# Last mixture of experts: weights in 4 MB units of 32768-byte rows in four slots

## The reference

```
h    = normalised tokens (512 x 1024), modulated by a scale and a shift per feature
for e in 16 experts:                       # 64 tokens each
    a    = h[tokens of e]                  # 64 x 1024
    hid  = silu(a @ w1[e]) * (a @ w3[e])   # w1, w3: 1024 x 2048 (8 MB each)
    y    = hid @ w2[e]                     # w2: 2048 x 1024 (8 MB)
    out[tokens of e] += gate * y
```

## Time and profile before

| | us |
|---|---|
| runs shown | 2056.22, 2057.51, 2052.18 |
| their median | 2056.22 |
| the profiled execution | 2052.67 |
| its span, first to last instruction | 2050.9 |

### The profile page before, as it was taken

The page is one execution under the profiler, slowest core; times in us unless marked ns, Lnnn a source line. Parts: engine busy times, 40 slices in busy tenths (PEclk is TensorE's granted clock), DMA queues, the critical chain, the costliest instruction groups (busy, mean ns, idle before and its releaser), DMA issues.

```text
span 2050.9 us, 25928 instructions
## 1 busy us (share of the span) xinstructions
PE 1885.8 (92%) x10445; PEld 1161.5 (57%) x10445; DVE 811.7 (40%) x1405; ACT 506.5 (25%) x875; POOL 252.3 (12%) x188
## 2 busy tenths in 40 slices
PE   9999999989999989999999998898979889897987
PEld 7876897775555577889876343433434333343433
DVE  5886453454645567568944111201211110111113
ACT  6666563332222255311233000000000000000002
POOL 4660520001111120004301000000000000000000
PEclk9999999999999999999999999999999999999999
DMA  7442441058999972222264999999999999999994
GB/s 299 189 175 113 187 162 62 1 206 328 390 381 375 376 275 103 83 99 86 83 241 199 428 428 428 426 429 428 428 427 428 429 426 429 428 428 426 429 429 182
DMA packets 80939, 608.66 MB, mean 297 GB/s; under 512 B 8571, under 2 KB 27387, under 8 KB 35164
## 3 DMA queue, kind: packets, MB, share of 16 engines
q1 hardware_dynamic: 66252, 576.62, 68.8%
q10 hardware_dynamic: 11216, 18.61, 2.4%
q0 software_dynamic: 3392, 12.32, 1.6%
HBM read 608.83 MB, written 20.71 MB: 307 GB/s over the span
## 4 chain that ended last, share of the span: by engine, by line
PE 60%; DMA 25%; DVE 6%; ACT 4%; POOL 2%; issue 2%; SPq 1%; POOLq 0%; ACTq 0%; DVEq 0%
PE psum L982 58%; DMA arena<-in_w 13%; DMA ring<-in_w 11%; DVE arena L2397 2%; PE psum L980 2%; DVE arena L2405 1%; DMA arena<-in_stream 1%; DVE weights_low L2397 1%; ACT weights_high L1893 1%; ACT arena L1875 1%; SPq L651 1%; DVE arena_low L2397 0%; ACT arena L1943 0%; POOL arena L870 0%; POOL arena L960 0%
## 5 line engine op out<-in xcount | busy, mean ns | idle before, releaser
L982 PE MATMUL psum<-ring,arena 128*64 128x512 f32 (+1 forms) x3064 | 858.8, 605 | 98.7 <-DMA ring<-in_w 65.2
L982 PEld LDWEIGHTS psum<-ring,arena 128*64 128x64 f32 x3064 | 280.6, 139 | 616.4 <-issue 605.1
L982 PE MATMUL psum<-arena 128*64 128x512 f32 (+5 forms) x1506 | 454.5, 457 | 9.9 <-ACT arena L1875 4.2
L1875 ACT ACTIVATE arena<-psum 128x512 f32<-128x512 f32 (+2 forms) x154 | 83.3, 550 | 706.9 <-PE psum L982 662.5
L982 PE MATMUL psum<-arena_low,weights_high 128*128 128x512 f32 (+1 forms) x704 | 249.6, 373 | 0.0
L982 PE MATMUL psum<-features_high_part,weights_high 128*128 128x512 f32 x576 | 228.7, 397 | 9.4 <-ACT arena L1875 4.6
L982 PE MATMUL psum<-features_high_part,weights_low 128*128 128x512 f32 x576 | 226.0, 392 | 0.0
L982 PEld LDWEIGHTS psum<-arena 128*64 128x64 f32 (+2 forms) x1506 | 198.5, 164 | 44.0 <-issue 27.3
L2405 DVE SCALAR_TENSOR_TENSOR arena<-psum,modp,arena 128x512 f32<-128x512 f32 x64 | 48.1, 751 | 293.2 <-PE psum L982 288.0
L2397 DVE TENSOR_TENSOR arena<-psum,arena 128x512 f32<-128x512 f32 (+2 forms) x48 | 28.9, 603 | 327.4 <-PE psum L982 263.9
L2397 DVE TENSOR_TENSOR weights_low<-ring,weights_high 128x2048 fp32r<-128x2048 f32 (+1 forms) x47 | 109.9, 2342 | 82.9 <-ACT weights_high L1893 79.0
(11 more groups left out here) (340 smaller groups left out, 1913.9 us busy)
## 6 DMA issues: line engine op xcount, KB each, us to landing
ring<-in_w SPq DMA_DIRECT2D x136, 2048.0 KB, 23.3
ring<-in_moe SPq DMA_DIRECT2D x93, 1024.0 KB
arena<-in_w SPq DMA_DIRECT2D x40, 2048.0 KB, 27.6
ring<-in_stream SPq DMA_DIRECT2D x53, 1024.0 KB, 6.7
arena<-in_stream SPq DMA_DIRECT2D x16, 1024.0 KB, 4.8
ring<-in_w SPq DMA_DIRECT2D x16, 1024.0 KB, 25.5
arena<-in_w SPq DMA_DIRECT2D x16, 1024.0 KB, 27.4
in_spectra<-ring ACTq DMA_DIRECT2D x8, 1024.0 KB
```

Source lines behind the costliest of these rows:

```text
L982: ins_ = pe.matmul(o, lhs, rhs, start=start, stop=stop)
L1875: bk.emptied.inc(act.activation(dst, o, func, **more))
```

## The change

Units of the last mixture become 4 MB with rows of 32768 bytes, in four slots instead of eight: 16 MB in either kernel. A unit of `w1` or `w3` now holds four k (each partition four neighbouring rows), a unit of `w2` eight steps. The last 4 MB of each expert's `w2` arrive in three pieces: 2 MB in 16384-byte rows and two quarters of 1 MB in 8192-byte rows, each with a semaphore. The first four units are loaded as eight halves ahead of SP's loop, in the same order of slabs as before; `w1` of the next round is issued at the end of the loop's body. Since a slot needs two neighbouring regions, `arena` 1 and 2 hold it, and what lay in region 2 moves to region 3. The layouts of tokens, scale and shift follow by fours, and of the hidden values by eights.

```diff
-RING2 = 8
-WIDE = 2 * UNIT
+RING2 = 4
+WIDE = 4 * UNIT
...
-        x_sel_t = region(2, 1024, KD, P)
+        x_sel_t = region(3, 1024, KD, P)
...
-        moe2_slot = [two_units(BACK_SLOT), arena[:, 3, :]]
-        moe2_slot += [two_units(r) for r in (8, 0, 4, 6, 10)] + [arena[:, 1, :]]
-        freed_by = {2: HYIN_END + 1, 3: HYIN_END + 2, 4: HYIN_END + 3}
+        moe2_slot = [ring[:, r:r + 4, :].rearrange("p a n -> p (a n)") for r in (0, 4, 8)]
+        moe2_slot.append(arena[:, 1:3, :].rearrange("p a n -> p (a n)"))
+        first_halves = [(0, 1, 0), (3, 1, 0), (2, 0, HYIN_END + 1), (0, 0, HYIN_END + 2), (1, 0, HYIN_END + 3),
+                        (1, 1, 0), (2, 1, 0), (3, 0, 0)]
...
+            def ups(name, first):
+
+                for k in range(2):
+                    for e in range(2):
+                        load(rows_of(name, first + e, KD // 2 * k, KD // 2 * k + KD // 2, 4))
+
+            def downs(first):
+
                 for e in range(2):
+                    load(rows_of("w2", first + e, 0, KD // 2, 8))
+                rows_ = [rows_of("w2", first + e, KD // 2, KD, 8) for e in range(2)]
+                slots = [load(rows_[e][:, 0:WIDE // 2], WIDE // 2) for e in range(2)]
+                for quarter, landed in ((2, s_late), (3, s_later)):
+                    at = slice(WIDE // 4 * quarter, WIDE // 4 * quarter + WIDE // 4)
+                    for e in range(2):
+                        sp.dma_start(moe2_slot[slots[e]][:, at], rows_[e][:, at]).then_inc(landed[e], 16)
...
+            with sp.Fori(0, NE // 2 - 1) as i:
+                used.enter(i, 12)
+                ups("w3", 2 * i)
+                downs(2 * i)
+                ups("w1", 2 * i + 2)
+                used.leave(NE // 2 - 1)
+            ups("w3", NE - 2)
+            downs(NE - 2)
...
-                        if k % 2 == 0:
+                        if k % 4 == 0:
                             w = [unit(), unit()]
...
-                        if k % 2 == 1:
+                        if k % 4 == 3:
                             used()
                             used()
 
                 for n in range(4):
+                    if n % 2 == 0:
+                        read(bk_d, 2)
                     o = begin(bk_d)
...
-                for k in range(KD // 2):
+                for k in range(2):
                     w = [unit(), unit()]
-                    for a in range(4):
-                        last = k == KD // 2 - 1 and a == 3
-                        if k == KD // 2 - 1 and a == 2:
+                    for a in range(8):
+                        last = k == 1 and a == 7
+                        if k == 1 and a in (4, 6):
                             for e in range(2):
-                                pe.wait_ge(s_late[e], 16 * i + 16)
+                                pe.wait_ge((s_late if a == 4 else s_later)[e], 16 * i + 16)
...
             def columns_paired():
 
                 o = begin(bk_d)
-                for h in range(2):
-                    for a in range(2):
-                        pick = ident.rearrange("p (j a) -> p a j", a=2)[:, a, :]
+                for h in range(4):
+                    for a in range(4):
+                        pick = ident.rearrange("p (j a) -> p a j", a=4)[:, a, :]
...
-                    empty(take().rearrange("p (j a) -> p a j", a=4), hid2_part(n), ACT.Silu)
+                    empty(take().rearrange("p (j a) -> p a j", a=8), hid2_part(n), ACT.Silu)
```

More of the change, by code:

```diff
@@ L526, in build @@
         s_arrived2 = [sem(f"expert_arrived{r}") for r in range(RING2)]
-        s_late = [sem(f"expert_last_half{e}") for e in range(2)]
+        s_late = [sem(f"expert_third_quarter{e}") for e in range(2)]
+        s_later = [sem(f"expert_last_quarter{e}") for e in range(2)]
         s_used = sem("units_used")
@@ new lines, in _ @@
+            for slot_, half, freed in first_halves:
+                if freed:
+                    sp.wait_ge(s_used, uses_through(freed))
+                at = slice(WIDE // 2 * half, WIDE // 2 * half + WIDE // 2)
+                k, e = slot_ // 2, slot_ % 2
+                sp.dma_start(moe2_slot[slot_][:, at], rows_of("w1", e, KD // 2 * k, KD // 2 * k + KD // 2, 4)[:, at])\
+                    .then_inc(s_arrived2[slot_], 16)
+            used.n += 4
+            turn[0] += 4
+            with sp.Fori(0, NE // 2 - 1) as i:
[4 more added lines that the diff above has]
+                used.leave(NE // 2 - 1)
@@ L2317, in _ @@
                     split()
-                empty(take(), region(2)[:, n, :], bias=modg[:, n:n + 1], scale=modp[:, 16 + n:17 + n])
+                empty(take(), region(3)[:, n, :], bias=modg[:, n:n + 1], scale=modp[:, 16 + n:17 + n])
             for k in range(KD):
                 act.wait_ge(s_lnc, KD * ln_no[0] + k + 1)
-                act.activation(region(5)[:, k, :], region(2)[:, k, :], ACT.Square).then_inc(s_lnq, 1)
+                act.activation(region(5)[:, k, :], region(3)[:, k, :], ACT.Square).then_inc(s_lnq, 1)
             act.activation(tiny[0:1, 0, 6:7], zero[0:1, :], ACT.Sqrt)
@@ L2331, in _ @@
                 act.wait_ge(s_lnm, KD * ln_no[0] + k + 1)
-                act.activation(x[:, k, :], region(2)[:, k, :], ACT.Identity, bias=vcol("ln_b2", k),
+                act.activation(x[:, k, :], region(3)[:, k, :], ACT.Identity, bias=vcol("ln_b2", k),
                                scale=vcol("ln_g2", k)).then_inc(s_lno, 1)
@@ L2336, in _ @@
                 for t in range(ST):
-                    empty(take().rearrange("p (k j a) -> p k a j", k=2, a=2),
-                          h_tok[:, t, 512 * half:512 * half + 512].rearrange("p (k a j) -> p k a j", k=2, a=2),
+                    empty(take().rearrange("p (j a) -> p a j", a=4),
+                          h_tok[:, t, 512 * half:512 * half + 512].rearrange("p (a j) -> p a j", a=4),
                           bias=of_token(4)[:, t:t + 1], scale=of_token(3)[:, t:t + 1])
@@ L2986, in columns_paired @@
             def columns_paired():
-                o = take()[:, 0:2 * KD].rearrange("p (n a k) -> p n a k", n=2, a=2)
-                do(dve.tensor_copy(modp[:, 32:40].rearrange("p (k a) -> p a k", a=2), o[:, 0]))
-                done(dve.tensor_copy(modc[:, 24:32].rearrange("p (k a) -> p a k", a=2), o[:, 1]))
+                o = take()[:, 0:2 * KD].rearrange("p (n a k) -> p n a k", n=2, a=4)
+                do(dve.tensor_copy(modp[:, 32:40].rearrange("p (k a) -> p a k", a=4), o[:, 0]))
+                done(dve.tensor_copy(modc[:, 24:32].rearrange("p (k a) -> p a k", a=4), o[:, 1]))
             def router_tables():
@@ L3245, in _ @@
                     split()
-                stt(region(2)[:, n, :], x[:, n, :], ALPHA, region(2)[:, n, :], ALU.mult, ALU.add)\
+                stt(region(3)[:, n, :], x[:, n, :], ALPHA, region(3)[:, n, :], ALU.mult, ALU.add)\
                     .then_inc(s_res, 1)
```

52 lines of the change are left out of this document (19 added, 33 removed).

## The result

The changed kernel takes **2162.46 us**, median of 3 runs (2153.48 to 2168.35), against 2056.22 before: 1.0519 times as long, 95% interval 1.0492 to 1.0545, or 106 us. Its profiled execution took 2153.48 us (span 2151.8), 100.8 more than the profiled one of before. Slower was right; +11 us was ten times too small, and the time lies far outside the range of 2053 to 2083.

A forecast was written before the change was run, and what follows sets the result against it. Transfers were taken to bound the kernel, TensorE not far behind. The terms -5.7 + 9.0 + 4.0 + 2 + 1.7 summed to +11.0 us, median 2067.2 us, put down as 2066.5 us, with a range of 2053 to 2083 us.

The forecast's parts named there:

- What bounds the kernel: Last mixture, 45% of the span: transfers set the pace, a round taking 117.63 us, with TensorE not far behind.
- a, rows and transfers: Weight loads of the last mixture: fewer rows and transfers save 0.75 us a round, -5.7 us in all.
- b: Start of the last mixture: 4 MB slots are given back after the fourth k instead of the second, +9.0 us.
- c: End of the last mixture: the last work waits in units of 8 MB, ending 8.2 us after the last landing, +4.0 us.
- M3: Third of a round's six 8 MB pair landings, w3's first; its release was put 4 to 5.5 us before the next landing.
- d: Last mixture's rounds: with two pairs of slots, late releases cost 0.3 us a round, +2 us, bounds 0 to 17.
- M4: Fourth pair landing of a round, w3's second; its release was put 4 to 5.5 us before the next landing.
- M2: Second pair landing of a round, w1's second, put at 38.9 us after the previous round's last landing.
- 2.4 us to spare: Release of w1's first pair, said to come 2.4 us before the next landing; the need was put at 2 to 3 us.
- The clock argument: TensorE in w3: a 5.5 us gap brings the 1.2 GHz clock every time, 1.5 us more on M3's and on M4's matmuls.
- e, columns by fours: Records with modp and modc: 16 become 64, +1.7 us, lower bound 0 if later waits hide it.
- Rival B: Last mixture is slot-bound: half clock after each long gap gives slots back late, +26 us, 2082 us; 15%.

The follow-up runs named there:

- own_release_warm: own_release with 20 and 12 matmuls on constants before w3's two waits for units: 2077.81 us, ratio 1.0121.
- first_load_halved: own_release_warm with the first round's first pair of w3 loaded in halves, reload starting after two k instead of four: 2072.01 us, ratio 1.0083.
- own_release: The changed kernel with releases riding on the pair's own last matmuls (before w3, on an added small matmul): 2083.6 us, ratio 1.0137.
- half_work_32k: own_release with 256 of the 512 columns of each of the stage's weight matmuls left out: 2053.47 us, ratio 0.9991.
- half_work_16k: half_work_32k with each 4 MB load split into two transfers of 16384-byte rows: 2060.84 us, ratio 1.0034.
- late_between_w1_w3: own_release with only the release from w1 to w3 made late again, on w3's first matmul: 2120.66 us, ratio 1.0316.
- warm_gaps: The changed kernel, late release kept, with 32 matmuls on constants ahead of each of w3's two waits for units: 2156.56 us, ratio 1.05.

## Why the prediction was wrong, by its own steps

**What bounds the kernel.** Right for before. For the changed kernel it no longer holds: the chain from a landing to the next release, issue and landing bounds it, not the transfers.

**a, rows and transfers, -5.7.** Right: 0.9 us a round against 0.75. It appears in the changed kernel only under the other losses.

**b and c, start +9.0 and end +4.0.** Right in size: in own_release_warm, where no release is held behind a wait, w2's first end comes 1215.35 - 1200.86 = 14.5 us later, against 13 and a little for the empty queue. The changed kernel's first reload went out at 1122.36 against 1112.82, 9.5 us later. "TensorE will wait some 6 us" for M3 was 8.0 us. For c the traces have the last data and w2's last emptying: 2032 and 2039.60 in own_release_warm, 2019 and 2022.84 before, so some 4 us more. The cause of b is less sure than its size: first_load_halved, which undoes it, gave back 6 us by the medians and 2.3 at w2's first end.

**d, slots that come back late, +2, bounds 0 to 17.** This is the step that failed. Its premise, "their releases come 4 to 5.5 us before the next landing, enough", put the release at the pair's last matmul. It comes at the next one. For M4 that is a transpose, and the premise holds. For M3 it is the first matmul of M4, and for M2, which the text can have meant only among its "two other releases" at 0.3 us, the first of M3: neither can run before the next landing. The text had counted the matmuls up to the release, but not asked which instruction carries it and what that instruction waits for. Had it done so, the traces had the price. Two matmuls at half clock, 2.0 us (the earlier trace rows show the half clock after gaps of 2.7 us), the issue, and the slow start of an empty queue come between landing and landing, twice a round: 24 us instead of 19.4. It measured 8.8 us a round (own_release against the changed kernel). All of d, put down as 0.3 us a round, is the last four rows below, 11.9 us:

| us a round | predicted | measured | by |
|---|---|---|---|
| rows and transfers (a) | -0.75 | -0.9 | half_work_32k, half_work_16k |
| release held behind w3's first wait | 0 | 3.6 | late_between_w1_w3, own_release |
| release held behind w3's second wait | 0 | 5.2 | the changed kernel, late_between_w1_w3 |
| half clock after gaps | in 0.3 | 1.9 | own_release, own_release_warm |
| rest (short lead of M1's release and else) | in 0.3 | 1.2 | what is left |

From 117.4 these give 128.4. The differences are those of one profiled execution each, and by the medians 3.6 would be 4.6 and 1.9 would be 0.7, so only the sum of the two held releases is firm. The row of w3's second wait also holds w2's first release, which was changed with it and by the windows above adds nothing. The last row is near 117.75 - 116.71 = 1.0 us, own_release_warm against half_work_32k. In own_release_warm the rate still drops to 262 GB/s from 1244 to 1246 and to 270 from 1304 to 1306, beside M1's and M4's reloads (1244.41 and 1302.08): the "2.4 us to spare" were not enough to keep the queue full. In the changed kernel's first round, 23.8 - 14.5 = 9.3 us are late release and half clock: the landings stand at 1145.52, 1169.71 and 1194.85, 24.2 and 25.1 us apart instead of 19.4.

**The direction** was no luck. Without the failed step the change is still slower: by 30 us in own_release and by 23 in own_release_warm, against the medians of the kernel before beside them. Both lie above the +11 of the sum. By the profiled executions the +17 of own_release_warm is 14.5 at the start and end and 7 x 0.3 for the rounds; what the medians add to it is open.

**The clock argument** in d was right in direction: gaps of 8 us bring the granted clock to 0.50. The Trainium skill (TensorE: Matmul & The Clock Gate, Why this matters for your kernels) wants no long idle gaps between bursts of matmuls, and these rows agree. In warm_gaps filling two of the gaps was worth some 6 us by the medians, with intervals that overlap.

**e, columns by fours, +1.7.** The size was nearly right and its weight wrong. `columns_paired` took 581.67 to 584.96 = 3.3 us instead of 0.78: 2.5 more, a little above the 2.3 of the dearer estimate. The next common point, ACT's row L1942, starts at 772.49, and at 772.84 before: later waits hide it all, and it is worth 0, the lower bound on record. The trace of the changed kernel at both points:

```profile
581.67 0.28 PE L1001 MATMUL psum<-modp,ident 128*32 128x2 f32 x2 [0.17 <-DVE arena L2420]
...
584.96 5.35 PE L1001 MATMUL psum<-ring,arena 128*64 128x512 f32 x16
...
772.49 0.81 ACT L1942 ACTIVATE arena<-arena,modc,modp 128x512 f32<-128x512 f32 x1 [2.68 <-DVE arena L2420]
```

**The rivals.** Rival B had the right place, slots, and the wrong agent: the clock is worth 13 us of 101 by the profiled executions and 6 by the medians, not the whole. Its counter-argument ("M3's and M4's releases have 4 us") was the false premise again, for M3, so forecast and rival shared the error, and the range with them.

## What to carry to other kernels

Before slots are made fewer and larger, look up which instruction carries each release and what **that** instruction waits for: a release that rides on the first use of the next buffer costs nothing while more transfers are queued, and empties the queue once the next buffer is the only one in flight. The sign in the trace here was a reload that went out 2 to 3 us behind each landing. The edit that puts the release on the last use is a few lines. Even then, the same bytes in half as many slots cost a start and an end in the coarser unit (14.5 us here), against 6 to 7 us that the larger rows and fewer transfers gave.

## What the runs showed of the hardware

**An empty queue has its own price.** In the second round a pair of 8 MB took 21.2 to 21.3 us from its second issue to its landing on an empty queue. On a full one a pair came every 19.4 us (a sixth of half_work_32k's round of 116.7). That is about 2 us that a full queue hides. The Trainium skill (SBUF — State Buffer, The DMA setup-cost knee) gives a fixed part of roughly 2 us a transfer. These rows agree with it where the queue is empty, and the earlier trace rows do not where it is full.

**Rows of 32768 bytes**, in half as many transfers, moved 431 GB/s against 427 for 16384, with the share at 1.00 and 1.01: 1% and no more.

**A low clock cost nothing where transfers bound.** The half_work kernels, with half the matmul columns, ran the stage at a mean clock of 0.81 to 0.82 and kept their DMA share at 1.00 and 1.01.
